# Sparse attention's minima and exponentials one pair ahead, value products two behind, and longer filling matmuls

## What is computed

```python
def rms_norm(x, w, eps=NORM_EPS):
    xf = x.astype(jnp.float32)
    y = xf * lax.rsqrt(jnp.mean(xf * xf, axis=-1, keepdims=True) + eps)
    return (y * w.astype(jnp.float32)).astype(x.dtype)
...
        sc = jnp.einsum('bhgqd,bhnd->bhgqn', qn, k_cmp).astype(f32) * scale
        pc = _masked_softmax(sc, cmp_end[None, :] <= t_pos[:, None])
        o_c = jnp.einsum('bhgqn,bhnd->bhgqd', pc, v_cmp)
...
        ps = _masked_softmax(ss.reshape(bsz, C_KV_HEADS, C_GROUP, QBLK, n_sel * SLC_BLK) * scale, ms)
        o_s = jnp.einsum('bhgqm,bhqmd->bhgqd', ps,
...
        pw = _masked_softmax(sw, mw)
        o_w = jnp.einsum('bhgqk,bhkd->bhgqd', pw, vwb.astype(f32))
        return (gt[..., 0:1] * o_c + gt[..., 1:2] * o_s + gt[..., 2:3] * o_w).astype(qr.dtype)
```

## Time and profile before

| what | us |
|---|---|
| median of 3 runs | 4383.24 |
| the profiled execution's own time | 4386.43 |
| its span, first to last instruction | 4384.5 |
| PE busy, by the profile | 4059.3 |
| DVE busy | 1581.4 |
| ACT busy | 1294.8 |

### The profile page before, as it was taken

The page is one execution under the profiler, slowest core; times in us unless marked ns, Lnnn a source line. Parts: engine busy times, 40 slices in busy tenths (PEclk is TensorE's granted clock), DMA queues, the critical chain, the costliest instruction groups (busy, mean ns, idle before and its releaser), DMA issues. The chain is left out here.

```text
span 4384.5 us, 56341 instructions
## 1 busy us (share of the span) xinstructions
PE 4059.3 (93%) x21923; PEld 3386.8 (77%) x21923; DVE 1581.4 (36%) x2731; ACT 1294.8 (30%) x2253; POOL 224.5 (5%) x187
## 2 busy tenths in 40 slices
PE   8999999999899999999997899999998879999999
PEld 5787786787677887678765776787776669999998
DVE  2365534232336553423235554332333421111122
ACT  2364533231236453323123322222213311111111
POOL 0150100000015010000000000000000000000000
PEclk9998989999999898999998899999996779999999
DMA  3100011221210001122120001232230015555544
GB/s 123 43 1 1 0 39 67 96 86 58 84 43 1 1 0 39 67 96 86 58 87 34 1 20 68 83 103 82 83 107 1 20 63 178 200 215 178 217 168 144
DMA packets 54647, 333.47 MB, mean 76 GB/s; under 512 B 7601, under 2 KB 8497, under 8 KB 23521
## 3 DMA queue, kind: packets, MB, share of 16 engines
q1 hardware_dynamic: 51904, 324.95, 21.1%
q0 software_dynamic: 2592, 6.49, 0.6%
HBM read 326.17 MB, written 4.19 MB: 75 GB/s over the span
## 5 line engine op out<-in xcount | busy, mean ns | idle before, releaser
L501 PE MATMUL bank<-high 128*128 128x512 f32 x2480 | 976.6, 394 | 44.0 <-DVEq L591 22.8
L502 PE MATMUL bank<-low,high 128*128 128x512 f32 x2480 | 973.8, 393 | 0.0
L503 PE MATMUL bank<-high,low 128*128 128x512 f32 x2480 | 972.7, 392 | 0.0
L501 PEld LDWEIGHTS bank<-high 128*128 128x128 f32 x2480 | 471.5, 190 | 150.2 <-DVEq L591 25.6
L503 PEld LDWEIGHTS bank<-high,low 128*128 128x128 f32 x2480 | 471.0, 190 | 98.8
L502 PEld LDWEIGHTS bank<-low,high 128*128 128x128 f32 x2480 | 471.4, 190 | 97.9
L561 DVE TENSOR_TENSOR low<-weight_ring,high 128x2048 fp32r<-128x2048 f32 (+1 forms) x144 | 319.3, 2218 | 546.0 <-ACT high L518 546.0
L3124 PE MATMUL bank<-chosen,glu_ring 128*128 128x176 f32 x2816 | 424.5, 313 | 0.0
L3124 PEld LDWEIGHTS bank<-chosen,glu_ring 128*128 128x128 f32 x2816 | 421.3, 190 | 0.0
L518 ACT ACTIVATE high<-weight_ring 128x2048 fp32r<-128x2048 f32 (+1 forms) x144 | 266.7, 1853 | 267.1 <-PE bank L503 233.1
L239 PE MATMUL bank<-filler 128*128 128x512 f32 x819 | 245.0, 442 | 24.0 <-PEq L172 23.3
(11 more groups left out here) (501 smaller groups left out, 4772.2 us busy)
## 6 DMA issues: line engine op xcount, KB each, us to landing
glu_ring<-in_w_expert SPq DMA_DIRECT2D x88, 1024.0 KB, 5.2
weight_ring<-in_w_ff SPq DMA_DIRECT2D x64, 1024.0 KB, 5.0
down_ring<-in_w_expert_down SPq DMA_DIRECT2D x64, 704.0 KB, 5.1
weight_ring<-in_w_in SPq DMA_DIRECT2D x22, 1024.0 KB, 4.7
weight_ring<-in_w_ffe SPq DMA_DIRECT2D x22, 1024.0 KB, 4.9
weight_ring<-in_w_downe SPq DMA_DIRECT2D x16, 704.0 KB, 4.1
weight_ring<-in_w_ino SPq DMA_DIRECT2D x11, 1024.0 KB, 4.9
weight_ring<-in_w_ine SPq DMA_DIRECT2D x9, 1024.0 KB, 4.9
```

Of the source, the lines that this page charges most:

```text
L501: nc.tensor.matmul(mem.bank[b][:, :], whole, high[:, k, :], start=(k == 0), stop=False)
L502: nc.tensor.matmul(mem.bank[b][:, :], whole, low[:, k, :], start=False, stop=False)
L503: last = nc.tensor.matmul(mem.bank[b][:, :], rest, high[:, k, :], start=False, stop=(k == kt - 1))
```

## The change

1. Longer fillings: norms 30 to 42, the adding norm 60 to 84, `add_norm`'s last 30 to 42, `linear` 5 to 12 where the first weights were loaded but not split ahead (the two output projections of the even and odd layers), `compress` 30 to 52, and 4 and 8 new ones at the attention's start.
2. In the attention, DVE's minima and ACT's exponentials of pair q+1 stand ahead of the copies of pair q. The copies of pair q stand in the iteration of q.
3. PE's value products run two pairs behind, `turned` has 6 buffers for 4.
4. `weigh`, `first_part` and `other_parts` stand behind the copies; the last two move to odd pairs.

```diff
-            fill_in(nc, mem, mem.bank[1], 30 if add_to is None else 60)
+            fill_in(nc, mem, mem.bank[1], 42 if add_to is None else 84)
...
-            fill_in(nc, mem, mem.bank[2], 30)
+            fill_in(nc, mem, mem.bank[2], 42)
...
-                fill_in(nc, mem, mem.bank[n_banks - 1], 5)
+                fill_in(nc, mem, mem.bank[n_banks - 1], 5 if primed == SPLIT else 12)
...
-            fill_in(nc, mem, turn_banks[0], 30)
+            fill_in(nc, mem, turn_banks[0], 52)
...
-                if q >= 2:
-                    act.wait_ge(applied, q - 1)
-                nc.scalar.activation(turned[:, 2 * q % 4, 0:width], turn_banks[0][:, 0:width], ACT.Copy) \
+                if q >= 3:
+                    act.wait_ge(applied, q - 2)
+                nc.scalar.activation(turned[:, 2 * q % 6, 0:width], turn_banks[0][:, 0:width], ACT.Copy) \
...
             exponent_c(0)
+            exponent(0)
             for q in range(n_pairs):
                 j, at = divmod(q, per_tile)
-                exponent(q)
+                if q + 1 < n_pairs:
+                    exponent(q + 1)
...
-                if q >= 1:
-                    take_turned(q - 1)
...
                 if q >= 7 and q % 2:
                     take_rows((q - 7) // 2)
-                if q >= 4 and q % 2 == 0:
-                    first_part((q - 4) // 2)
-            take_turned(n_pairs - 1)
+                take_turned(q)
+                if j + 1 < tiles and at == 3:
+                    exponent_c(j + 1)
+                if q >= 5 and q % 2:
+                    first_part((q - 5) // 2)
...
             rotate(0)
+            fill_in(nc, mem, turn_banks[0], 4)
             pe.wait_ge(rot_taken, 1)
             score_c(0)
+            fill_in(nc, mem, mem.bank[6], 8)
...
-                if q >= 1:
-                    apply(q - 1)
+                if q >= 2:
+                    apply(q - 2)
...
+                if q >= 1:
+                    pe.wait_ge(high_taken, q)
                 fill_in(nc, mem, turn_banks[0], 1)
                 transposed(q)
+            apply(n_pairs - 2)
             apply(n_pairs - 1)
...
+            top(0)
             for q in range(n_pairs):
                 j, at = divmod(q, per_tile)
-                top(q)
+                if q + 1 < n_pairs:
+                    top(q + 1)
+                if j + 1 < tiles and at == 2:
+                    top_of_c(j + 1)
+                take_turned(q)
+                if j + 1 < tiles and at == 3:
+                    mask_c(j + 1)
                 if q >= 4 and q % 2 == 0:
                     weigh((q - 4) // 2)
-                if q >= 1:
-                    take_turned(q - 1)
...
-                if q >= 4 and q % 2 == 0:
-                    other_parts((q - 4) // 2)
-            take_turned(n_pairs - 1)
+                if q >= 5 and q % 2:
+                    other_parts((q - 5) // 2)
```

More of the change, by code:

```diff
@@ L2433, in sparse_attention @@
     with buffers(nc, q_rot=[P, 2, SEQ], turn=[P, SEQ], values=[P, TT, 2 * C_KV, wide], vc=[P, C_KV, wide],
-                 gate=[P, TT, C_HEADS * N_BRANCH], probs=[P, 4, SEQ], turned=[P, 4, SEQ], probs_c=[P, 2, TT, N_CMP],
+                 gate=[P, TT, C_HEADS * N_BRANCH], probs=[P, 4, SEQ], turned=[P, 6, SEQ], probs_c=[P, 2, TT, N_CMP],
                  top_c_rows=[P, 2 * TT], turned_c=[P, 2, 2, SEQ], tops=[P, 2 * n_pairs], weights=[P, n_groups, 2, N_BRANCH],
@@ L2537, in _ @@
                         scale_query(j + 1)
-                    elif at == 3:
-                        exponent_c(j + 1)
                     elif at in (4, 6):
@@ L2614, in apply @@
                     for b in range(t + 1):
-                        last = nc.tensor.matmul(product(g, h, 1 + branch), turned[:, (2 * q + h) % 4, b * P:(b + 1) * P],
+                        last = nc.tensor.matmul(product(g, h, 1 + branch), turned[:, (2 * q + h) % 6, b * P:(b + 1) * P],
                                                 values[:, b, branch * C_KV + kv_of(j), :], start=(b == 0), stop=(b == t))
@@ L2716, in take_turned @@
                 dve.wait_ge(turn_out, 2 * q + 2)
-                if q >= 2:
-                    dve.wait_ge(applied, q - 1)
+                if q >= 3:
+                    dve.wait_ge(applied, q - 2)
                 width = (t + 1) * P
-                nc.vector.tensor_copy(turned[:, (2 * q + 1) % 4, 0:width], turn_banks[1][:, 0:width]).then_inc(low_taken, 1)
+                nc.vector.tensor_copy(turned[:, (2 * q + 1) % 6, 0:width], turn_banks[1][:, 0:width]).then_inc(low_taken, 1)
             def weigh(g):
```

## The result

| what | before | after |
|---|---|---|
| median of the runs, us | 4379.89 (5 runs) | 4349.28 (5 runs, 4343.94 to 4357.52) |
| ratio, with its 95% interval | | 0.9928 (0.9906 to 0.9949) |
| repeated, us | 4377.75 (19 runs) | 4350.37 (5 runs) |
| ratio of the repetition | | 0.9922 (0.9893 to 0.9952) |
| the profiled execution's own time, us | 4386.43 | 4343.94 |

The kernel is faster by 0.7%: about 31 us in the first job, 27 in the repetition. The forecast was 4334 with a range of 4312 to 4366. The time lies in the range and on the right side, 15 us above the forecast.

A forecast was written before the change was run, and what follows sets the result against it. PE was taken as the bound, with its idle time and half-clock time left to gain. Attention -39, norms -9.2, `linear` -6, output projections -3, adding norm +9.2, second pass -1.3 sum to -49.3, giving 4334 us, range 4312 to 4366.

The forecast's parts named there:

- The removed wait: Attention: exponentials are done before PE's score matmuls ask, so the 15 us that PE idles for ACT go.
- The new waits, 13.4 us: Attention: PE waits for late part steps and second exponentials, 3.0 us in each of three tiles, more in the last.
- The low clock that is left, 24 us at a cost of 11: Attention: new waits and the start leave one or two half-clock stretches, 24 us, costing 11; the attention gains 39.
- the sum of 125: Attention: PE's work all at the full clock, 57 us from the half-clock part plus 68 already full.
- The norms' fillings, -9.2: Norms: 42 fillings just fit beside DVE's work; four places give back half their low clock behind them, -9.2 us.
- The other fillings, -6 and -3: Stretches where `linear` follows gain 6 us from less low clock; the two output projections gain 3 us.
- The adding norm, +9.2: Adding norm, two places: 24 more fillings bring PE to the barrier 4.6 us after DVE, twice, +9.2 us.
- the -1.3 of the sum: Second pass: the sums behind the adding norm gain back some 1.3 us as their gap shrinks from 3.0 to 2.1.
- Outside the attention: All terms but the attention's: norms -9.2, `linear` -6, output projections -3, adding norm +9.2, second pass -1.3 us.
- the second case: Rival, attention: each new wait takes the clock down, only idle time goes, attention -8, total about 4365; chance 0.15.
- (third): Rival, attention: exponentials do not get ahead because `probs` has 4 buffers, PE waits as now, some 4368; chance 0.04.
- (fourth): Rival, slower: the clock stays at half through the whole attention, +43 there, total 4416; chance 0.05.

The follow-up runs named there:

- part steps first: Against the kernel after: ACT's first parts and DVE's part steps of odd pairs ahead of that pair's copies; 4318.22 us, ratio 0.9859 (with fillings as before, 4336.92 us).
- rows first: Kernel with part steps ahead of copies and 60 adding-norm fillings, plus ACT's copy of turned rows ahead of exponentials at odd pairs; 4317.28 us, ratio 0.9851.
- 60 fillings: Kernel after with the adding norm's fillings back at 60 for 84, the norms' 42 kept; 4318.53 us, ratio 0.9863.
- 72 fillings: Kernel after with 72 fillings in the adding norm for 84; 4325.41 us, ratio 0.9888.

## Why the prediction was right, and where it was off

It was right in code, sign and range, and its sum was 15 us too favourable. By its own steps:

- **The removed wait.** Forecast: 15 us of idle time for ACT's exponentials gone. Shown: 14.7 us of it with the fillings alone, none after.
- **The new waits, 13.4 us.** The mechanism was right (L2610 for DVE's part steps); the size was too high. At place 6 it measured 0.51 + 0.24 us for 0.85 + 0.65, at place 4 0.22 + 0.32 for 0.5 + 0.7, in the last tile 0.78, 0.36 and twice 1.78. The counting let PE reach the value products too early and summed both waits in full. The filling behind ACT's copy of the rows, 3.6 us, it missed. All idle time in the attention was 16.6 us for a forecast 22.3.
- **The low clock that is left, 24 us at a cost of 11: this is the step that failed.** There were 50 us in one execution and 62 in the other. At the prediction's ratio, 1 - 1/1.85 = 0.46, they cost 23 and 28.5 us, 12 to 17 more than forecast. In the first, the idle time was 5.7 lower and the work at the full clock 2.7 higher (167.3 - 23 - 16.6 = 127.7 for 125; the 12 new fillings at 0.23 are such work, and the sum of 125 left them out). That gives the attention's miss of 9 us, -30.2 for -39; in the second it is 14, -24.6. I had the right cause in hand, a new wait as long as the stop of 0.84 us, and gave it one or two stretches on a feeling. Each tile has two such places and the last tile four. The stop of 0.78 us in the last tile is followed by 17.1 us of half clock in all seven traces that have the change's order, and the last stop of some 1.8 us by 13.7 or 17.1 in six of them; in the seventh a stretch of 27.3 begins behind the first of the two such stops. With the part steps first L2610's stops for DVE's rows are gone but for 0.4 us, and 7.9 us stay low; the same move gives about the same with either set of fillings.
- **The norms' fillings, -9.2.** Confirmed by itself: the four groups of L647 are shorter by 1.69, 2.90, 2.91 and 1.69 us, 9.2 together, and none has any low clock left. But in the first pass 3.4 us of half clock stand in the next phase instead, behind its first gap, and with the norms' counts taken back, those of the adding norm included, the kernel's median does not change.
- **The other fillings, -6 and -3.** From the `add_norm`'s sums to the next norm's, where a `linear` stands, 1.5 and 1.2 us are gained for the 1.8 forecast each, and in the stretch with the third one 1.9 for 1.4. From the attention's end to the next norm's sums, the odd layer's output projection, it is 2.4 us. The even layer's can't be told from the rest of its stretch.
- **The adding norm, +9.2.** Confirmed: 4.45 and 4.30 us of idle time on DVE, 4.3 us each between 60 and 84 fillings. The adding norm as a stretch grew by 1.7 us less than that each time, with less of it at half clock; the -1.3 of the sum counted such a gain for the second pass alone.
- **Outside the attention**, all told, -10.3. It was -12.5 in the first profiled execution and -10.3 in the second (-34.9 of span less 24.6). The agreement of the sum says less than it seems, since its parts moved by more (next section).
- **From one execution to the median.** The profiled execution of before lay 3.2 us above its median and that of after 5.3 below, so -42.5 in the profiles is -34 against the median shown (4383.24). The second execution, at the median of its kernel, has the 15 us: 14.4 of them are the attention's.

The trace of before had a warning on the failed step. The prediction leans on a stop of 0.84 us behind which no low stretch began. The same trace has a stop of 0.83 us, and behind it, from 3412.0 on, the 17 us at 0.50 of the earlier trace rows:

```profile
3409.55 0.70 PE L2583 MATMUL bank<-u,q_rot 64*128 64x256 f32 x4 [0.83 <-ACT probs L2490]
```

Its low stretches also begin sooner behind a stop than the prediction read, by 1.4 to 2.8 us, and eight times. Of the signs that the prediction named, one missed: it asked for an attention of 150 to 165 us at a clock above 0.85, and the two executions have 167.3 us at 0.85 and 172.9 at 0.82.

The rivals: of the second case (4365, the low time stays near 111 us) about half came true, 50 to 62 us; the exponentials do get ahead (third); the clock is not low throughout (fourth). The Trainium skill's sentence that transposes do not engage the full clock ("TensorE: Matmul & The Clock Gate", part 4 on the PE-mode transpose) did not decide this stretch, in which other matmuls stand between them: with its 160 transposes it ran at 0.97 once the part steps were out of the way.

What stays open: why stops of 0.83 and 0.99 us, which are left six times with part steps first, are followed by almost no low clock there, while one of 0.78 us in the order of the change is followed by 17 us every time, and two of 0.94 and 1.27 us by 34 and 27 us in the kernel with the rows first. What stands between the stops differs, and so does the time at which they fall; no run here separates the two.

## What to carry to other kernels

Where PE is the bound, read how much of a stretch is at half clock before counting its idle time: here one move of two calls took away 42 us of low clock, worth 19 us, and 4 us of idle time. When an order is written by hand, put work whose inputs are there ahead of work that waits for the engine being fed, and move what makes its inputs along with it. Count fillings against the instruction that they cover, place by place, and time a kernel in several executions: what one edit gives can be smaller than what it shifts elsewhere.

## What was not expected of the hardware

Stretches of the program in which no instruction was changed took different times in different kernels, with more or less of them at half clock. In the repetition of the kernel after, most had the same length to 0.5 us. The second pass, from its first sums to those of its `add_norm`, took 658.8 us after and 658.5 in the repetition, 652.8 with 60 fillings and 645.6 with 72, with 107.2, 106.9, 94.4 and 72.2 us at half clock. The even layer took 482.6 us after and in the repetition, 475.4 with 60 fillings, 477.2 with 72, and 474.4 with part steps first, whose code up to there is that of the kernel after. Between these kernels each us of half clock goes with 0.38 to 0.49 us of length, near the 0.46 of the ratio of 1.85; the even layer with 72 fillings stands apart, with 5.4 us for 6.8.

Since single executions of a kernel also fell elsewhere (4328.79 of the kernel after, whose others lie above 4343; 4350.61 with 72 fillings, whose others lie below 4333), an edit can show some 20 us more or less in this kernel than its own terms say: of the 31 us of the 60 fillings 22 are of that kind, and of the 31 of part steps first 8.

It is not the time at which a stretch starts, counted from the start of the execution, that decides. The even layer of the kernel with two fillings in each pair starts 8.1 us earlier than in the kernel after and has the same length and the same low time; so have the repetition and the fillings alone, 1.6 and 2.4 us earlier. With part steps first it starts 0.10 us earlier and is 8.2 us shorter:

```profile
2194.82:2677.39 482.57, 426.28 (x2494) 338.33 (x2494) 221.57 (x362) 138.54 (x230) 0.00 (x0) 0.90 0.11 37
```
```profile
2202.82:2677.20 474.38, 419.35 (x2494) 332.06 (x2494) 221.63 (x362) 138.69 (x230) 0.00 (x0) 0.92 0.11 37
```

The lengths go rather with the fillings ahead of the stretch: 482.6 us in four of the five traces with 42 in the norms and 84 in the adding norm, 475.4, 475.5 and 478.7 in the three with 42 and 60. The fifth with 84, part steps first, shows that this does not settle it either. What decides stays open.
